# Thirty-two late tokens take their scores from gathered rows of U instead of sixteen

## What is computed

```python
# xt: tokens x 1024; q: 8 heads x 2 halves; 128 keys a half; 16384 experts
v1, i1 = top_k(s1, 16); v2, i2 = top_k(s2, 16)
top, pos = top_k(v1[..., :, None] + v2[..., None, :], 16)    # 16 experts a head
eidx = i1 * 128 + i2;  g = softmax(top)
act = gelu(einsum("td,thkd->thk", xt, expert_u[eidx]))       # a score per token and expert
y = einsum("thk,thkd->td", act * g, expert_v[eidx])
```

## Time and profile before

| | |
|---|---|
| median of 3 runs | 1573.88 us |
| profiled execution | 1572.96 us, span 1571.2 us |
| granted TensorE clock | 0.997 of full (2.4 GHz) |
| busy: PE, DVE, POOL, ACT | 98%, 73%, 68%, 40% of the span |
| scores from tiles of U, main part | about 401 to 994 us |
| sums of values | 994 to about 1505 us |
| moved by DMA | 420.46 MB, 268 GB/s over the span |

### The profile page before, as it was taken

One profiled execution on the slowest core, in us unless ns is written; L12 is line 12 of the kernel. 1 busy time (PEld: TensorE's weight loads), 2 busy tenths in 40 slices (PEclk: granted clock), 3 DMA queues, 4 the chain that ended last, 5 costly groups with the idle time before them and its releaser, 6 DMA issues.

```text
span 1571.2 us, 24832 instructions
## 1 busy us (share of the span) xinstructions
PE 1537.1 (98%) x8585; PEld 1387.2 (88%) x8585; DVE 1154.0 (73%) x2386; ACT 623.8 (40%) x936; POOL 1074.7 (68%) x564
## 2 busy tenths in 40 slices
PE   6999999999999999999999999999999999999998
PEld 6987887788899999999999999888888888888886
DVE  5898563787999943299999993577767776776746
ACT  3334752201333333446655564433333333333331
POOL 6544314454599898897766765788887878778853
PEclk9999999999999999999999999999999999999999
DMA  7222203321599999899999997999999999999961
GB/s 279 82 81 95 94 28 124 135 81 56 174 356 334 316 339 324 296 322 359 350 345 359 355 334 240 325 347 362 357 364 358 364 357 352 346 342 349 347 222 54
DMA packets 168852, 420.46 MB, mean 268 GB/s; under 512 B 15936, under 2 KB 90048, under 8 KB 163920
## 3 DMA queue, kind: packets, MB, share of 16 engines
q1 hardware_dynamic: 125568, 256.02, 46.3%
q0 software_dynamic: 39168, 142.62, 25.2%
q10 hardware_dynamic: 4048, 21.01, 3.4%
HBM read 367.08 MB, written 52.51 MB: 267 GB/s over the span
## 4 chain that ended last, share of the span: by engine, by line
PE 73%; DMA 0%; SPq 0%; issue 0%; DVE 0%; ACT 0%; DVEq 0%
PE psum L1627 33%; PE psum L379 11%; PE psum L384 11%; PE psum L378 11%; PE psum L1611 5%; PE psum L240 1%; PE psum L241 1%; PE psum L231 1%; DMA u_raw<-in_u_t 0%; SPq L1460 0%; PE psum L271 0%; PE psum L1599 0%; ACT acts L1691 0%; DVE e_gate L2048 0%; DVE e_nT_lo L2035 0%
## 5 line engine op out<-in xcount | busy, mean ns | idle before, releaser
L1527 POOL TENSOR_TENSOR u_lo<-u_raw,u_hi 128x1024 fp32r<-128x1024 f32 x220 | 545.2, 2479 | 176.0 <-ACT u_hi L1686 172.3
L1686 ACT CAST u_hi<-u_raw 128x1024 fp32r<-128x1024 f32 x252 | 263.7, 1048 | 296.7 <-PE psum L1627 247.4
L378 PE MATMUL psum<-hn_hi,u_hi 128*128 128x368 f32 x1024 | 340.0, 332 | 3.5 <-PEq L137 2.1
L379 PE MATMUL psum<-hn_lo,u_hi 128*128 128x368 f32 x1024 | 337.1, 329 | 0.0
L1627 PE MATMUL psum<-u_hi,s_whi 128*128 128x512 f32 x768 | 298.0, 389 | 0.9 <-ACT acts L1691 0.9
L1627 PE MATMUL psum<-u_hi,s_wlo 128*128 128x512 f32 x768 | 297.9, 389 | 0.0
L1627 PE MATMUL psum<-u_lo,s_whi 128*128 128x512 f32 x768 | 297.9, 389 | 0.0
L378 PEld LDWEIGHTS psum<-hn_hi,u_hi 128*128 128x128 f32 x1024 | 192.4, 188 | 4.1 <-issue 2.4
L379 PEld LDWEIGHTS psum<-hn_lo,u_hi 128*128 128x128 f32 x1024 | 192.2, 188 | 0.0
L384 PE MATMUL psum<-hn_hi,u_lo 128*128 128x368 f32 x1024 | 191.5, 329 | 0.0
L1560 POOL DMA_INDIRECT s_vrows<-in_v_t,s_v_row x128 | 169.7, 1325 | 26.4 <-issue 25.1
(11 more groups left out here) (327 smaller groups left out, 2666.5 us busy)
## 6 DMA issues: line engine op xcount, KB each, us to landing
u_raw<-in_u_t SPq DMA_DIRECT2D x128, 512.0 KB
u_raw<-in_v_t SPq DMA_DIRECT2D x128, 512.0 KB
act_scratch<-acts SPq DMA_DIRECT2D x128, 192.0 KB
scores<-act_scratch SPq DMA_DIRECT2D x32, 768.0 KB
gate_scratch<-s_gtile ACTq DMA_DIRECT2D x10, 2048.0 KB, 10.4
scores<-gate_scratch SPq DMA_DIRECT2D x32, 640.0 KB
m_w_raw<-in_w_in SPq DMA_DIRECT2D x10, 1024.0 KB, 4.9
m_w_raw<-in_w_q SPq DMA_DIRECT2D x8, 1024.0 KB, 4.8
```

The source lines that it names most:

```text
L378: pe.matmul(out, hi[:, d * P:(d + 1) * P], dense(hn_hi, d), start=(d == 0), stop=False)
L379: pe.matmul(out, hi[:, d * P:(d + 1) * P], dense(hn_lo, d), start=False, stop=False)
L1527: pool.tensor_tensor(lo[:, s, :], raw[:, s, :], hi[:, s, :].bitcast(F32), ALU.subtract).then_inc(lo_ready[s], 1)
L1686: act.copy(hi[:, s, :], raw[:, s, :]).then_inc(hi_ready[s], 1)
```

## The change

```diff
-DOTS_FREE = 32
+DOTS_FREE = 48
-XT = 16
+XT = 32
 XG = P // XT
 XK = PAIRS // XG
 DS = DT - XT
@@ scalar engine, the bodies
-            steps(0)
-            steps(1)
+            for j in range(3):
+                steps(j)
             for s in range(U_RING):
                 act.wait_ge(dotted[s], x_till // U_RING + (s < x_till % U_RING))
             act.activation(x_dots[:, :], x_dots[:, :], ACT.Gelu).then_inc(x_gelu, 1)
             act.wait_ge(x_gelu, 1)
             act.dma_start(xa_dram, x_dots[:, :]).then_inc(xa_stored, 16)
-            steps(2)
+            steps(3)
             act.wait_ge(xa_stored, 16)

             def take_back(g):
+                if g >= XG:
+                    return
                 act.dma_start(x_acts[g * XK:(g + 1) * XK, :], xa_dram[g * XT:(g + 1) * XT, :].rearrange("t k -> k t"), allow_slow_non_contiguous=True).then_inc(xa_back, 16)

-            steps(3, also=take_back)
-            with act.Fori(4, n_body - 1) as j:
-                steps(j)
+            steps(4, also=take_back)
             steps(n_body - 1, keep=True)
```

## The result

The changed kernel takes 1601.84 us in the median of 4 runs (1600.88 to 1602.39), beside 1573.54 (1571.84 to 1574.2) for the kernel before on the same chip: a ratio of 1.0182, 95% interval 1.017 to 1.0195. It is slower by 1.8%, on the side that was forecast (1597 us), 4.8 us above the number and inside the range of 1588 to 1607. The profiled execution took 1601.79 us with a span of 1600.0 us, where before's span was 1571.2: 28.8 us to account for.

The account below looks back on a forecast made before the run. TensorE bound the kernel with almost no margin; after the change POOL would. 25.3 + 5.1 - 10.7 + 2.5 + 1 - 0.3 = 22.9 us on 1572.96, plus 0.9 to the median: 1597 us, range 1588 to 1607.

Parts of the forecast that it names:

- The gain: TensorE's tiles: 352 columns save 0.16 us each, 20.5 us over 128 tiles if TensorE stayed the bound.
- What POOL issues: Tiles 15 to 59: POOL needs 4.18 us a tile, above TensorE's 3.84; tiles 34 to 60 take 5.1 us more.
- The wait in front of it: Up to tile 33: gathers wait for retrieval's dots eight earlier, so tile 33 ends 25.3 us later.
- The walk: Stepping through POOL's new list against dot times up to tile 33: low 33 ends at 554.8.
- dots where they are: Assumption in retrieval: dots 0 to 27 keep their old times, dot 27 done at 545.50.
- Tiles 61 to 127: Behind tile 60 TensorE sets the pace again: 67 x 0.16 = 10.7 us less.
- DVE in the bodies: Late dots span 21 body steps and DVE falls behind: 2.5 us more, ends 0 and 5.
- DMA, +1: Transfers in tiles 34 to 60: 39.4 MB cost 1 us more, ends 0 and 10.
- The rival of a DMA bound: DMA becomes the bound in tiles 34 to 60: at 319 GB/s 10 us on top, 1607; chance 0.08.
- Only POOL's pace: Rival: no gather waits for dots, POOL's pace alone costs time, about 1578 us; chance 0.04.
- TensorE stays the bound: Rival: POOL's lead of some 6 us covers its delays, all 20.5 us come, 1553; chance 0.05.
- the signs: Expected in the trace: gathers waiting for DVE until 546, TensorE waiting 20 to 30 us for L1527, gates near 729.

Follow-up runs that it names:

- e6_half: The changed kernel with tiles 4 to 127 of U loaded by half: 1598.15 us.
- e5_psum: The changed kernel with one input of DVE's subtraction L1867 taken from a copy in PSUM: 1594.38 us.
- e2_table: The kernel before, still 368 columns and 144 gathers, with the changed kernel's steeper POOL list up to tile 72: 1611.3 us.
- e8_tail_half: The changed kernel with the 16 added gathers behind the bodies, two a tile, and tiles 4 to 127 of U loaded by half: 1562.6 us.
- e1_ramp: The changed kernel with POOL's old list up to tile 34 and the remaining 44 gathers beside tiles 35 to 63: 1580.42 us.
- e3_narrow: The kernel before with dense products of 352 columns and nothing else, leaving out sixteen tokens' dense scores: 1558.97 us.
- e7_split: The changed kernel with POOL's old list up to tile 34, 8 added gathers in tiles 34 to 63 and 8 behind the bodies: 1572.87 us.

## Why the prediction was right, and where it was not

- **The gain: right.** A tile in the bodies follows after 5.62 us, as (columns + 32) / 2400 had it for a width that no row showed. Outside the bodies tiles 61 to 71 stand some 3.87 us apart, not 3.84.
- **What POOL issues: right.** From the end of low 33 (562.40) to that of low 60 (675.1) are 112.7 us; the sum had 113.1. e6_half excludes DMA as the cause.
- **The wait in front of it: right in its mechanism, too small by 8.0 us.** The walk had gather 16 wait for dot 8, gather 17 for dot 9, and so on to gather 35. POOL's timeline after shows it:
```profile
468.24 2.41 POOL L1527 TENSOR_TENSOR u_lo<-u_raw,u_hi 128x1024 fp32r<-128x1024 f32 x1
477.70 1.04 POOL L1539 DMA_INDIRECT h<-in_u_rows,s_u_row  x1 [7.05 <-DVE s_dots L1807]
481.77 1.00 POOL L1539 DMA_INDIRECT h<-in_u_rows,s_u_row  x1 [3.03 <-DVE s_dots L1807]
...
520.62 1.04 POOL L1539 DMA_INDIRECT h<-in_u_rows,s_u_row  x1 [6.08 <-DVE s_dots L1807]
...
553.98 1.04 POOL L1539 DMA_INDIRECT s_more_row<-in_u_rows,s_u_row  x1 [1.14 <-DVE s_dots L1807]
...
559.99 2.41 POOL L1527 TENSOR_TENSOR u_lo<-u_raw,u_hi 128x1024 fp32r<-128x1024 f32 x1
```
Low 18 ends at 470.65 (472.1 in the walk) and gather 16 goes at 477.70 (478.1 in it). But gather 35 goes at 553.98, not 546.3, and low 33 ends at 562.40, not 554.8, so tile 33 is 33.25 us late instead of 25.3. The step that failed is the assumption "dots where they are". I froze the times of dots 8 to 27, because DVE had no time to spare; retrieval took 7.8 us longer. That is 8.5 us on L1867 and 2.9 on L1835 less 5.1 on L1885, all three short DVE instructions that finish only when a low part of POOL has ended, and 1.5 us of later rows. That L1867's time hangs on its second input in SBUF is shown by e5_psum; for the two casts the blocking is read from the rows only. Which of them meets a low part seems a matter of phase: in the kernel before L1885 met them, after the change L1867 and L1835 did, and e2_table, with the same list and wider products, repeats that and the length of retrieval. I had seen the pattern at the late dot of the earlier trace rows and priced it in the bodies only, where it is a small matter.
- **Tiles 61 to 127.** The sum had -10.7 for the columns and +2.5 for DVE in the bodies, together -8.2; measured -9.1. The 67 x 0.16 came, less 1.6 us. About 1.1 us of it is lost at one place, the first gates, which wait 0.80 us for DVE, behind a late row; in the 48 body steps behind them hardly anything (TensorE is busy 249.19 of 250 us). DVE's lead was enough for the late dots' extra cost, so the +2.5 was not due, and what was lost came from a place that the sum had at nothing: POOL's lead covered the low parts of tiles 64 to 71 but not quite the row that the first gates need. The chain of the kernel after at the first gates:
```profile
706.80 7.94 DMA s_late_rows<-in_u_rows,s_u_row
714.76 1.22 DVE s_late_rows L1807
717.16 2.64 DVE scores L1934 x8
719.81 1.14 DVE scores L1936
```
- **DMA, +1: nothing.** The share is 0.99 at 347 GB/s in the stretch from 560 to 600, but e6_half says that this is not what paces the tiles. The rival of a DMA bound falls for tiles 34 to 60. It holds behind the bodies when rows are put there at two a tile (e8_tail_half).
- **Only POOL's pace.** The nearest run, e1_ramp, gives 1580 where the rival said about 1578, but that is no proof of its price: there tile 33 was 1.5 us earlier than in the kernel before, tiles 34 to 60 took 8.0 us more, and tiles 61 to 127 gave nothing back (355.1 us against 354.8), where the rival counted on their 10.7. The case was not this one.
- **TensorE stays the bound** would have needed 1553; e3_narrow with no added gather at all reaches 1559, so even its best case was some 6 us dearer than I had it.

The terms as measured: +33.25 (25.3), +4.7 (5.1), -9.1 (-8.2), DMA and start 0 (+0.7): 28.8 us in the profiled execution, where the sum had 22.9. The 8.0 us of the first term were in part made up by the others, and 0.9 more by the step from the profiled execution to the median, which was not there after the change. So a forecast only 4.8 us off owes something to luck: one term was off by 8.

Of the signs, the waiting gathers came as said (7.05 us before gather 16, the last wait at 553.98), but TensorE waited 36.7 us for L1527, not 20 to 30, and the gates that were to come near 729 came at 738.2, later by the 8.0 and the 1.1 us above. The sign "retrieval's dots at other times than before", listed as one of being wrong, is there.

Not settled is the start: retrieval began 3.0 us later in e5_psum's profiled execution than in the changed kernel's, so its tile 33 was only 3.4 us earlier where retrieval was 6.4 us shorter. Over all ten traces retrieval begins between 399.94 and 404.84 us, though the edits touch next to nothing of what stands ahead of it, and the cause was not tried. So times at which something ends, compared between two single traces, carry a few microseconds that no edit made; the length of a stretch does not. Nor was it tried to take the blocking from L1835 and L1885.

## What to carry to other kernels

An engine that runs a hand-written order with a ring couples everything behind it to the ring's slowest consumer. Before making such a list steeper, walk it against the consumer's times; here the same sixteen gathers cost 43 us beside retrieval (1601.84) and 7 behind the bodies (1565.99), both against 1558.97 without them. A stretch in which the producer seems idle may be the lead on which the next one lives (e1_ramp and e7_split suggest it). And in such a walk the consumer's times are not constants: ask which of its instructions share something with the engine that has been moved.

## What was not expected of the hardware

- **Short VectorE instructions are blocked by POOL's work for some ten times their own length.** L1867 (128x128, two inputs in SBUF) took 0.29 us free and up to 3.15 beside a gather's issue and a low part, and ended about 0.15 us after the low part each time. With one input in PSUM it took 0.292 on average, and 0.29 inside a low part. The Trainium skill (SBUF — State Buffer, Who interferes with whom) states this exclusion for two SBUF inputs against a GpSimd instruction that reads SBUF, and the run agrees. Not explained is that the longest ones began some 0.6 us before the low part, 0.46 us into the gather's issue, when the same instruction took 0.29 us at 447.69 in the kernel before, 0.31 us into an issue.
- **Casts of one input too.** L1835 took 3.27 us at 511.43 and ended at 514.70, 0.17 us after a low part; L1885 took 2.25 and 2.78 us in the kernel before. The Trainium skill (SBUF — State Buffer, Who interferes with whom) says that copy and cast can take the ports that they share with GpSimd when their operands meet certain conditions. That fits the rows, but no run here moved their operands. The dots (L1807 with one input in PSUM) stayed at 1.21 us on average in the same stretch.
- **TensorE's granted clock fell where it had waited.** It is 1.00 in the stretches of the earlier trace rows, and 0.89 and 0.83 on average from 480 to 560 us after the change, so part of that time was at the lower of its two levels (1.2 of 2.4 GHz). In PE's timeline the eight products behind a wait of 9.40 us took 2.71 us; behind a short wait they take 1.55:
```profile
528.13 2.71 PE L384 MATMUL psum<-hn_hi,u_lo 128*128 128x352 f32 x8 [9.40 <-POOL u_lo L1527]
...
675.12 1.55 PE L384 MATMUL psum<-hn_hi,u_lo 128*128 128x352 f32 x8 [0.59 <-POOL u_lo L1527]
```
TensorE was waiting for POOL in that stretch anyway, so little can have been lost by it; what it cost was not tried. From 560 us on the clock is at 1.00 again. Where TensorE has work to go on with it does cost: the gates behind e7_split's wait of 3.4 us took 3.19 us, where those of the changed kernel behind 0.80 us took 2.05.
